# A two-layer decoder trunk on one Trainium2 core: the first layer's up projection of the embedding rows is computed in the routing stage instead of the combine stage

## What is computed

```python
hn = rmsnorm(h, g_mix[0])
h = h + pool_mixer(hn, pool_w[0], pool_scale[0])          # mixing stage
h = h + hierarchical_moe(rmsnorm(h, g_ffn[0]), ...)       # routing, experts; added in combine
gate = sigmoid(rmsnorm(h, g_ple[0]) @ w_ple_gate[0])      # combine
h = h + gate * (p[0] @ w_ple_up[0])                       # combine; p[0] is (4096, 256)
k, v = shared_kv(h, g_kv, w_k, w_v, cos, sin)             # combine
q = rope(rmsnorm(h, g_mix[1]) @ w_q[0])                   # combine
```

## Time and profile before

| | us |
|---|---|
| median of 3 executions (range) | 5211.05 (5208.74 to 5211.11) |
| the profiled execution: its time | 5216.1 |
| the profiled execution: span of the instructions | 5214.0 |
| mixing, from about | 15 to 288 |
| routing of layer 0 | 288.8 to 373.8 |
| experts of layer 0 | 375 to about 1570 |
| combine (first PE matmul to last) | 1606.8 to about 2563 |

### The profile page before, as it was taken

How to read it: one execution, slowest core, us unless ns; L and a number is a source line. 1 busy time by engine, 2 the same in 40 slices (tenths; PEclk the granted TensorE clock), 3 DMA queues, 4 the chain that set the end, 5 groups by cost and what they waited for, 6 DMA issues and landing times. The chain is left out here.

```text
span 5214.0 us, 89612 instructions
## 1 busy us (share of the span) xinstructions
PE 4651.2 (89%) x29188; PEld 2939.8 (56%) x29253; DVE 2864.2 (55%) x5895; ACT 1946.7 (37%) x2834; POOL 1569.0 (30%) x1159
## 2 busy tenths in 40 slices
PE   7937999999994999999689999955999999996999
PEld 6925676666672444444256666634666766663444
DVE  5674444444444445444378888874444444444665
ACT  6814443343423221222145555513344343332333
POOL 1104444443421111111033333313444443431332
PEclk9968999999997999999889999977999999998999
DMA  6729999999967555555366677728999999886997
GB/s 215 278 76 317 307 310 300 302 285 299 287 202 206 144 153 143 151 147 139 82 157 173 174 181 181 176 59 269 306 302 300 308 284 310 277 255 189 223 214 164
DMA packets 1247970, 1152.90 MB, mean 221 GB/s; under 512 B 944016, under 2 KB 955280, under 8 KB 1247888
## 3 DMA queue, kind: packets, MB, share of 16 engines
q1 hardware_dynamic: 1201808, 984.09, 65.3%
q0 software_dynamic: 46080, 167.79, 10.4%
HBM read 696.63 MB, written 228.59 MB: 177 GB/s over the span
## 5 line engine op out<-in xcount | busy, mean ns | idle before, releaser
L726 POOL TENSOR_TENSOR ex_w_lo<-ex_raw,ex_w_hi 128x2048 bf16<-128x2048 f32 x192 | 780.2, 4091 | 1170.1 <-ACT ex_w_hi L784 1170.1
L784 ACT ACTIVATE ex_w_hi<-ex_raw 128x2048 bf16<-128x2048 f32 x384 | 707.2, 1900 | 522.8 <-PE ex_ps_y L110 189.0
L888 PE MATMUL ex_ps_gate<-ex_xT,ex_w_hi 128*128 128x0 bf16 x2048 | 573.1, 280 | 165.4 <-DMA ex_xT<-ex_xrow 133.8
L890 PE MATMUL ex_ps_gate<-ex_xT,ex_w_lo 128*128 128x0 bf16 x2048 | 573.4, 280 | 0.0
L889 PE MATMUL ex_ps_gate<-ex_xT,ex_w_hi 128*128 128x0 bf16 x2048 | 573.2, 280 | 0.0
L888 PE MATMUL ex_ps_up<-ex_xT,ex_w_hi 128*128 128x0 bf16 x2048 | 560.5, 274 | 0.0
L889 PE MATMUL ex_ps_up<-ex_xT,ex_w_hi 128*128 128x0 bf16 x2048 | 559.9, 274 | 0.0
L890 PE MATMUL ex_ps_up<-ex_xT,ex_w_lo 128*128 128x0 bf16 x2048 | 559.5, 273 | 0.0
L852 DVE TENSOR_TENSOR ex_aT<-ex_silu,ex_ps_up 128x384 bf16<-128x384 f32 x256 | 141.7, 554 | 723.5 <-PE ex_ps_up L890 549.8
L868 DVE COPY ex_y<-ex_ps_y 128x512 f32 x324 | 224.0, 691 | 567.2 <-PE ex_ps_y L110 510.4
L108 PE MATMUL ex_ps_y<-ex_w_hi,ex_aT 128*128 128x512 bf16 x1296 | 493.2, 381 | 6.6 <-DVE ex_aT L856 6.5
(11 more groups left out here) (351 smaller groups left out, 9474.7 us busy)
## 6 DMA issues: line engine op xcount, KB each, us to landing
ex_raw<-in_w_exp_gate SPq DMA_DIRECT2D x128, 1024.0 KB, 10.4
ex_raw<-in_w_exp_up SPq DMA_DIRECT2D x128, 1024.0 KB, 13.0
ex_raw<-in_w_exp_down SPq DMA_DIRECT2D x128, 1024.0 KB, 7.2
y_rows<-ex_y SPq DMA_DIRECT2D x162, 512.0 KB, 3.0
cb_hin<-h_mid SPq DMA_DIRECT2D x64, 512.0 KB, 3.8
mix_x<-in_x SPq DMA_DIRECT2D x32, 512.0 KB, 4.6
h_mid<-mix_h SPq DMA_DIRECT2D x32, 512.0 KB, 5.3
y_rows<-mix_zeros SPq DMA_DIRECT2D x32, 512.0 KB, 6.0
```

The costliest lines, as they stand in the source:

```text
L726: eng.tensor_tensor(w_lo[u][:, w], raw[:, c, :], w_hi[u][:, w], ALU.subtract).then_inc(lo_done, 1)
L784: act.activation(w_hi[u][:, c * WCHUNK:(c + 1) * WCHUNK], raw[:, c, :], ACT.Copy).then_inc(hi_done, 1)
L888: pe.matmul(out, hi, x_hi, start=j == 0, stop=False)
L890: mm = pe.matmul(out, lo, x_hi, start=False, stop=j == KD - 1)
```

## The change

Three places.

Mixing: SP also loads the tile of p of step s+1 (128 KB), stores the turned tile of step s-2 to a DRAM tensor `pT_rows` (128 KB, 1 KB per row), and issues the DMA transpose of tile s-1. ACT rounds p to bf16 at the end of its step (high part, 128x256), DVE subtracts (low part) at the end of its step.

Routing, layer 0 only: SP loads `w_ple_up` (2 x 512 KB) and `pT_rows` (4 x 1 MB); ACT makes the weights' high part and POOL the low part; PE does the 32 up products in the gaps of the routing's own matmuls: tiles 0 to 5 ahead of the counts, 6 to 12 ahead of the chunk list, 13 to 16 and then one ahead of each of the eight batches, and tiles 25 to 31 behind the last. ACT copies each half from PSUM, SP stores the tile (512 KB) to `up_rows`.

Combine: no p, no `wu`, no up product. `up_rows` is loaded per tile (512 KB) and DVE reads it in L1338's place. The weight jobs are 24 instead of 26 (4, 4, 16 for ACT and DVE; 8, 4, 12 for SP). Gate, q and k/v products have PSUM tiles of their own, with the waits changed to match.

```diff
@@ pool_phase: SP, at the end of its step
+                if has(s + 1):
+                    u = (r + 1) % 2
+                    wait(sp, pl_done, s)
+                    sp.sem_inc(turn_open, 1)
+                    sp.dma_start(p_in[u][:], p_t[s + 1]).then_inc(p_ld[u], 16)
+                if has(s - 2):
+                    sp.wait_ge(p_turned, 16 * (s - 1))
...
+                if has(s - 1):
+                    u = (r - 1) % 2
+                    sp.wait_ge(pl_done, s)
...
+                    sp.dma_start(pT[u][:], ph[u][:].rearrange("p h d -> p (h d)"), transpose=True).then_inc(p_turned, 16)
@@ ACT and DVE, at the end of their steps
+                    act.wait_ge(p_ld[u], done(s, u))
+                    wait(act, p_turned, 16 * (s - 1))
+                    act.activation(ph[u][:, 0, :], p_in[u][:], ACT.Copy).then_inc(ph_done, 1)
...
+                    dve.wait_ge(ph_done, s + 1)
+                    dve.tensor_tensor(ph[u][:, 1, :], p_in[u][:], ph[u][:, 0, :], ALU.subtract).then_inc(pl_done, 1)
@@ route_phase: ACT
+            def take_up(t0, t1):
+                for t in range(min(t0, tiles), min(t1, tiles)):
+                    for h in (0, 1):
+                        act.wait_ge(up_mm, 2 * t + h + 1)
+                        if h == 0:
+                            wait(act, up_st[t % UP], 16 * (t // UP))
+                        act.activation(up_out[t % UP][:, 512 * h:512 * h + 512], ps_up[h][:], ACT.Copy).then_inc(up_done, 1)
...
+            take_up(0, 2)
             act.wait_ge(e_in, 1)
             act.activation(ex[:], ex[:], ACT.Exp).then_inc(e_out, 1)
+            take_up(2, 6)
             act.wait_ge(e_in, 2)
             act.activation(ediff[:], ediff[:], ACT.Exp).then_inc(e_out, 1)
+            take_up(6, NT)
@@ route_phase: PE
+            def up(t0, t1):
+                for t in range(min(t0, tiles), min(t1, tiles)):
+                    if t % PIECE == 0:
+                        pe.wait_ge(pT_ld[t // PIECE], 16)
...
+                    for h in (0, 1):
...
+                        wait(pe, up_done, 2 * t + h - 1)
...
+            wait(pe, wu_lo_done, KPLE if tiles else 0)
+            up(0, 6)
             pe.wait_ge(ranked, 1)
...
+            up(6, 13)
             pe.wait_ge(listed, 1)
...
+            up(13, 17)
             for b in range(2 * NT // B):
+                up(17 + b, 18 + b)
                 pe.wait_ge(hot_done, b + 1)
...
+            up(17 + 2 * NT // B, NT)
@@ combine_phase
-        jobs += [([(A["w_ple_up"][layer], 0, D)], k, None, wu) for k in range(KPLE)]
...
-        ps_gate, ps_up = (ps[0], ps[2]), (ps[1], ps[3])
-        ps_q, ps_kv = (ps[4], ps[0]), ps[1]
+        ps_gate, ps_q, ps_kv = (ps[0], ps[1]), (ps[2], ps[3]), ps[4]
...
-                    dve.wait_ge(up_mm, 2 * s + h + 1)
+                    dve.wait_ge(up_ld[u], done(s, u))
...
                     gate(0)
-                    if isinstance(s, int) and s == 0:
-                        pe.wait_ge(w_lo_done, GU)
-                    up(0)
                     gate(1)
-                    up(1)
```

More of the change, by code:

```diff
@@ L230, in pool_phase @@
         zeros = m.sb("zeros", [P, D])
+        p_in = [m.sb(f"p_in{u}", [P, PLE]) for u in (0, 1)]
+        ph = [m.sb(f"ph{u}", [P, 2, PLE], BF16) for u in (0, 1)]
+        pT = [m.sb(f"pT{u}", [P, 2 * KPLE, P], BF16) for u in (0, 1)]
         ps_pool = m.ps("pool", [P, KD, P])
@@ L485, in route_phase @@
         part = m.sb("part", [P, 2, MAX_TILES])
+        UP = 3
+        PIECE = 8
+        tiles = NT if layer == 0 else 0
+        wu = m.sb("wu", [P, 2, KPLE, D], BF16)
+        wu_raw = [m.sb(f"wu_raw{k}", [P, D]) for k in range(KPLE)]
+        pT = [m.sb(f"pT{i}", [P, PIECE, 2, KPLE, P], BF16) for i in range(NT // PIECE)]
+        up_out = [m.sb(f"up_out{i}", [P, D]) for i in range(UP)]
+        ps_up = [m.ps(f"up{h}", [P, 512]) for h in (0, 1)]
+        wu_ld, pT_ld = ([m.sem(f"{n}{i}") for i in range(k)] for n, k in (("wu_ld", KPLE), ("pT_ld", NT // PIECE)))
+        up_st = [m.sem(f"up_st{i}") for i in range(UP)]
+        wu_hi_done, wu_lo_done, up_mm, up_done = m.sems("wu_hi_done wu_lo_done up_mm up_done")
+        up_t = C.up_rows.rearrange("(t p) d -> t p d", p=P)
         ps_before = m.ps("before", [P, NT, NE])
@@ L492, in route_phase, with _ @@
         block = stack.enter_context(nc.Block())
+        @block.sync
+        def _(sp):
+            for k in range(KPLE if tiles else 0):
+                sp.dma_start(wu_raw[k][:], A["w_ple_up"][layer][k * P:(k + 1) * P, :]).then_inc(wu_ld[k], 16)
+            for i in range(tiles // PIECE):
+                sp.dma_start(pT[i][:].rearrange("p t h k n -> p t (h k n)"),
+                             C.pT_rows[i * PIECE:(i + 1) * PIECE].rearrange("t p n -> p t n")).then_inc(pT_ld[i], 16)
+            for t in range(tiles):
+                sp.wait_ge(up_done, 2 * t + 2)
+                sp.dma_start(up_t[t], up_out[t % UP][:]).then_inc(up_st[t % UP], 16)
+            for i in range(UP):
+                wait(sp, up_st[i], 16 * len(range(i, tiles, UP)))
@@ L494, in _ @@
+        @block.gpsimd
+        def _(pool):
+            for k in range(KPLE if tiles else 0):
+                pool.wait_ge(wu_hi_done, k + 1)
+                pool.tensor_tensor(wu[:, 1, k, :], wu_raw[k][:], wu[:, 0, k, :], ALU.subtract).then_inc(wu_lo_done, 1)
         @block.scalar
         def _(act):
+            def take_up(t0, t1):
[5 more added lines that the diff above has]
+                        act.activation(up_out[t % UP][:, 512 * h:512 * h + 512], ps_up[h][:], ACT.Copy).then_inc(up_done, 1)
+            for k in range(KPLE if tiles else 0):
+                act.wait_ge(wu_ld[k], 16)
+                act.activation(wu[:, 0, k, :], wu_raw[k][:], ACT.Copy).then_inc(wu_hi_done, 1)
+            take_up(0, 2)
@@ L1156, in step @@
                     sp.dma_start(hin[u][:], h_t[t]).then_inc(h_ld[u], 16)
-                    wait(sp, pl_done, t - 1)
-                    sp.dma_start(p_in[u][:], p_t[t]).then_inc(p_ld[u], 16)
+                    if not mid_:
+                        sp.dma_start(up_in[u][:], up_t[t]).then_inc(up_ld[u], 16)
                 if head:
@@ L1180, in step @@
                     sp.dma_start(h3_t[s], h3[u][:]).then_inc(h3_st[u], 16)
+                    if load:
+                        sp.dma_start(up_in[u][:], up_t[s + 2]).then_inc(up_ld[u], 16)
                 if tail:
@@ L1233, in step @@
                     t = s + 1
-                    act.wait_ge(p_ld[v], done(t, v))
-                    wait(act, p_turned, 16 * t)
-                    act.activation(ph[:, 0, :], p_in[v][:], ACT.Copy).then_inc(ph_done, 1)
                     act.wait_ge(h2_done, t + 1)
@@ L1246, in step @@
                 if isinstance(s, int) and s < 1 and head:
-                    weights(*((5, 10) if s < 0 else (10, len(jobs))))
+                    weights(*((4, 8) if s < 0 else (8, len(jobs))))
                 if mid_:
@@ L2118, in __init__ @@
         self.kv_rows = dram("kv_rows", [T, 2 * KVW])
+        self.pT_rows = dram("pT_rows", [NT, P, 2 * KPLE * P], BF16)
+        self.up_rows = dram("up_rows", [T, D])
 def first_experts(nc, A, C):
     rot = Rotary(nc)
-    route_phase(nc, C, 0)
+    route_phase(nc, A, C, 0)
     experts_phase(nc, A, C, 0, rot)
```

81 lines of the change are left out of this document (41 added, 40 removed).

## The result

The changed kernel takes 5154.58 us (median of 4, 5152.90 to 5158.74) against 5209.90 for the kernel before (median of 4, 5204.06 to 5211.11); the ratio is 0.9892, with a 95% interval of 0.9879 to 0.9904. That is 55 us or 1.1% faster. The profiled execution took 5158.74 us, 5157.1 of it the span; the mean granted clock is 0.953 of full.

What follows compares the result with a forecast made beforehand. The prediction took PE to bound mixing and combine, and DVE the routing. Its terms, -77.7 - 10 + 8 + 1.5 + 23.5 = -54.7 us, gave 5156 us; the forecast's own range was 5138 to 5178, the stated range 5138 to 5184.

Steps and rivals of the forecast that it cites:

- Combine, steady: Steady combine steps: each of 30 loses 12 matmuls, 2.59 us, -77.7 us; x3T keeps 2.3 us of room.
- Rival (b): Combine: x3T comes late, landing 3.6 us later in each step, +39 us, 5195; chance 0.09.
- Combine, start: First tiles of combine: tile 1 and the weight loads behind its transpose come sooner, -10 us (5 to 11 gained).
- Mixing: Mixing steps: preparing p costs 0.25 us per step, +8 us in all (3 to 26).
- term for the split: Mixing: ACT's added 0.40 us ahead of hnT costs 0.2 us per step, less 0.1 of overlap.
- allowance for DMA: Mixing: queues wanted for 7.35 of 7.54 us, 97%, so some waiting expected; 0.25 us per step taken.
- price of a transpose: DMA queues: a transposed MB costs 5.4 us, a plain one 2.8; a step's added transpose 0.71 us.
- Rival (a): The mixing becomes bound by DMA, a step grows by 1.0 us: +32 instead of +8, 5180; chance 0.12.
- End of the mixing: Behind the last normalised rows: the last transpose and the store of its result add 1.5 us (0 to 4).
- Routing: Routing: the up products make DVE 3.2 us late and leave seven tiles at the end, +23.5 us (+20 to +35).
- Rival (c): Routing: PE stays at 1.2 GHz, 5.2 us per tile, +112 instead of +23.5, 5244; chance 0.03.
- The sum: Whole kernel: all terms together -54.7 us, the profiled 5216.1 becoming 5161.4, or 5156 against the median.

Runs made afterwards that it cites:

- e5: The changed kernel with x3 turned twice in combine, first into a spare tile, then into x3T; 5161.95 us.
- e6: The changed kernel with both halves of the split of p in the mixing on POOL instead of ACT and DVE; 5141.01 us.
- e7: The changed kernel with one more transpose of the split of p per mixing step, into a spare tile, and no more stores; 5183.65 us.
- e2: The changed kernel without the up products of tiles 25 to 31, rows of tiles 0 to 6 stored a second time instead; 5136.30 us.
- v2_ahead_late: The changed kernel with the first expert's weight loads issued in the routing and the last seven tiles' up products moved to the experts' start; 5135.21 us.

## Why the prediction was right, point by point

**Combine, steady.** Right, and so was its margin. The prediction took 12 matmuls, 2.59 us, off each of 30 steps; the mean period fell by 2.59 us (28.49 to 25.90). From the first to the last store of q_rows it is 78.0 us, where 77.7 were predicted. It left 2.3 us between the landing of x3T and its use; 2.5 us were found, and e5 shows that PE does begin to wait once the landing is later by that much. Rival (b) was a real limit at the distance stated, but the landing of 10.9 us that it leaned on is that of the first transpose of the stage and says nothing of the steady steps.

**Combine, start.** Predicted -10, measured -8.8 up to the first store of q_rows. The gap behind the first gate product ended 10.7 us sooner as the chain had it, and the gap ahead of the first q grew, from 3.34 to 8.04 us, which the prediction didn't name: it took the whole chain to x3T to come sooner with the gate product, and the landing of that transpose grew from 10.9 to 13.4 us. The stage as a whole is 86.7 us shorter by the two profiles each, 88.5 by the mean of all profiles of either form of combine but e5's (three and ten); -87.7 was predicted.

**Mixing.** Predicted +8, measured +5.2 (0.17 us per step instead of 0.25). The term for the split was right, 0.1 to 0.2 us, and e6 shows that the two operations are the whole cost; that it is ACT's, ahead of hnT, is what the waits say. What was mis-sized is the allowance for DMA: "that close to full I expect some waiting", and there was none. How full the DMA engines are was judged well enough to say that the traffic fits: e6 moves all of it in 7.52 us per step. It was not exact: the sum gave 97%, the share in the profile is 103.4%. The price of a transpose, more than that of plain transfers of as many bytes, stands by the shares; the experiments agree with a factor of two but don't isolate it. Rival (a), that late transposes make a step 1 us longer, didn't happen here and does with one more transpose per step (e7, 0.77 us); that e7's time is near the rival's 5180 is chance, since about half of its extra time is lost clock.

**End of the mixing.** Predicted +1.5, measured +1.3. The last transpose is issued at 286.15 and its store at 289.01:

```profile
286.15 1.27 SPq L312 DMA_TRANSPOSE mix_pT<-mix_ph  x1
289.01 0.34 SPq L302 DMA_DIRECT2D pT_rows<-mix_pT  x1
```

**Routing.** Predicted +23.5, measured +23.0, and the steps in between hold, in us behind the stage's start (predicted, then found): PE starts at 9.5, 9.0 to 9.4 (the record of its first matmul is missing); the counts start at 27.2, 27.5; they hold PE for 3.5, 3.4; DVE resumes at 30.9, 31.2; DVE is done at 88, 88.2; PE is through at 104.6, 104.6; the last store has landed at 108.5, 107.9; the experts start 109.0 behind the routing's start. The stretch at 1.2 GHz was a little longer than tile 0, some 14 matmuls instead of 12. One step was read wrongly and cost nothing: the prediction let DVE set the pace of the eight batches, but by its own terms PE, free for them at 63 and with 3.34 us per batch, is 0.6 us behind DVE at the last; in the trace PE has no gap there, and DVE waits 1.23 us for the last product. e2 confirms the division: 19.4 us of the stage for the seven tiles, 3.4 for the others. Rival (c) didn't happen: the clock rose 6 us after PE began and its mean over the stage was 0.92.

**The sum.** -54.7 was predicted and -55.3 measured by the medians. The stages that the change touches give 5.2 + 1.3 + 23.0 - 86.7 = -57.2 in the table, and the others of the table +6.6, most of it in the last stage and the experts of layer 1, in code that isn't changed. That the sum agrees to 1 us is partly luck: the spans of the two profiles of each kernel differ by 50.9 us in the mean, the medians by 55.3, and the mixing was 3 us cheaper than foretold. Single stages of unchanged code differ between profiles by up to 12 us (experts of layer 0: 1187 to 1194 us in eleven of them, experts of layer 1: 1207 to 1220 in all).

## What to carry to other kernels

Moving work from a stage that one engine bounds to a stage that another bounds pays to the amount of idle time there and no further: count the moved work against the receiving stage's own end, and the remainder (here seven of 32 tiles, 18 us) is the next thing to move, to a place where that engine is idle. Idle time behind a chain of loads, transposes and another engine's queue takes less than its length: of the 20 us by which v2_ahead_late shortened the routing, 13 were left behind the experts. The busy share of the DMA queue doesn't say whether a loop has room. Adding a known transfer does, but only if nothing waits for it and it stands behind the issues that matter; otherwise it measures the order of the queue as well.

## What the runs showed that was not expected

- The DMA share of the queue was 103.4% in the changed kernel at a period set by ACT, 107.0% in e6 at a period set by PE, and 104.4% in e7, where transposes landed too late for ACT. At these values it didn't tell a loop that DMA delays from one that it doesn't.
- With more transfers, SP's issues themselves can grow: that of the normalised rows took 0.33 us in the changed kernel and 1.12 at 166 us of e7.
- The granted clock fell to 0.5 for 3 to 7 us at places that differ from run to run; in both rows shown PE had gaps just before (5.8 of 7 us busy, 10.6 of 13). One such fall costs some 4 us (v2_ahead_late's steps of 8.9 and 10.9 us, the second tile of the last stage), as much as some of the effects studied here. At least two profiles of each kernel are needed before a stage difference of 5 us is put down to code.
